# Moving the high half of sixteen weight splits per layer from GpSimd to ScalarE in a two-layer encoder kernel

## The reference

```python
q = (xc @ w_query).reshape(-1, PEER_HEADS, 2, PEER_HALF)
s1, s2 = scores of both halves of q against sub_keys
v1, i1 = lax.top_k(s1, 16); v2, i2 = lax.top_k(s2, 16)
sv, pos = lax.top_k(all 256 sums v1 + v2, 16)
eidx = i1 * 128 + i2 at pos;  gate = softmax(sv)
act = gelu(einsum('thkd,td->thk', u_tab[eidx], xc))
y = einsum('thk,thkd->td', gate * act, v_tab[eidx])
x = layer_norm(ALPHA * x + y)
```

## Time and profile before

| | before |
|---|---|
| median of 3 runs | 3995.9 us (3995.53 to 3997.57) |
| profiled execution, its own time | 3997.35 us |
| its span in the trace | 3995.6 us |
| PE busy | 3807.2 us (95%) |
| DVE busy | 2760.0 us (69%) |
| POOL busy | 2505.9 us (63%) |
| ACT busy | 753.7 us (19%) |
| granted TensorE clock, mean | 0.983 |

### The profile page before, as it was taken

One profiled execution on the slowest core, in us unless ns is written; L12 is line 12 of the kernel. 1 busy time (PEld: TensorE's weight loads), 2 busy tenths in 40 slices (PEclk: granted clock), 3 DMA queues, 4 the chain that ended last, 5 costly groups with the idle time before them and its releaser, 6 DMA issues.

```text
span 3995.6 us, 54149 instructions
## 1 busy us (share of the span) xinstructions
PE 3807.2 (95%) x19024; PEld 3144.7 (79%) x19024; DVE 2760.0 (69%) x3953; ACT 753.7 (19%) x1305; POOL 2505.9 (63%) x1268
## 2 busy tenths in 40 slices
PE   6999996999999999999989999889999999999998
PEld 5778885778878888888877798667788788888886
DVE  7545999996998444444584559999789974444445
ACT  1551112331111111010115401133311110111101
POOL 5435574447777676766654455844577777667674
PEclk9999998999999999999999999999999999999999
DMA  3112234776554333333221123357764543333331
GB/s 143 53 64 93 93 137 140 230 221 235 188 189 158 125 128 116 115 126 120 90 86 64 72 90 111 127 164 220 235 225 178 199 143 121 116 126 126 115 115 74
DMA packets 224634, 546.56 MB, mean 137 GB/s; under 512 B 9728, under 2 KB 141056, under 8 KB 174976
## 3 DMA queue, kind: packets, MB, share of 16 engines
q1 hardware_dynamic: 46656, 335.57, 23.3%
q10 hardware_dynamic: 177856, 209.36, 16.1%
HBM read 442.12 MB, written 102.76 MB: 136 GB/s over the span
## 4 chain that ended last, share of the span: by engine, by line
PE 61%; DVE 30%; issue 6%; DVEq 1%; POOL 1%; ACT 1%; DMA 0%; ACTq 0%; SPq 0%; POOLq 0%
PE bank L1087 19%; PE bank L1089 19%; PE bank L1088 19%; DVE hot L988 3%; DVE Wl L1020 3%; DVE hot2l L993 2%; DVE hot L989 2%; DVE ki L908 2%; DVE Wf L1016 1%; PE bank L1210 1%; DVE pick L951 1%; DVE kv__78 L905 1%; DVE X L1037 1%; DVE pos L908 1%; DVE pick L948 1%
## 5 line engine op out<-in xcount | busy, mean ns | idle before, releaser
L383 POOL TENSOR_TENSOR part_l<-landing,part_h 128x1024 fp32r<-128x1024 f32 x632 | 1705.6, 2699 | 52.8
L380 POOL TENSOR_SCALAR part_h<-landing 128x1024 fp32r<-128x1024 f32 x632 | 810.3, 1282 | 1402.8 <-PE bank L1089 764.1
L1087 PE MATMUL bank<-XTh,part_h 128*128 128x512 f32 (+1 forms) x2688 | 1054.1, 392 | 11.1 <-DVE XTl L711 7.7
L1088 PE MATMUL bank<-XTl,part_h 128*128 128x512 f32 (+1 forms) x2688 | 1038.7, 386 | 0.0
L1089 PE MATMUL bank<-XTh,part_l 128*128 128x512 f32 (+1 forms) x2688 | 1038.4, 386 | 0.0
L1087 PE MATMUL bank<-part_h,Wh 128*128 128x512 f32 x2048 | 800.5, 391 | 9.9 <-DVE X L1037 7.1
L1089 PE MATMUL bank<-part_h,Wl 128*128 128x512 f32 x2048 | 797.3, 389 | 0.0
L1088 PE MATMUL bank<-part_l,Wh 128*128 128x512 f32 x2048 | 797.0, 389 | 0.0
L1087 PEld LDWEIGHTS bank<-XTh,part_h 128*128 128x128 f32 x2688 | 509.6, 190 | 110.0 <-POOL part_l L383 4.4
L1089 PEld LDWEIGHTS bank<-XTh,part_l 128*128 128x128 f32 x2688 | 508.6, 189 | 102.6
L1088 PEld LDWEIGHTS bank<-XTl,part_h 128*128 128x128 f32 x2688 | 509.6, 190 | 97.1 <-issue 0.5
(11 more groups left out here) (165 smaller groups left out, 3542.3 us busy)
## 6 DMA issues: line engine op xcount, KB each, us to landing
landing<-stream SPq DMA_DIRECT2D x316, 1024.0 KB, 4.8
dense_gates<-spill ACTq DMA_DIRECT2D x32, 2048.0 KB, 9.4
gate<-dense_gates ACTq DMA_DIRECT2D x64, 1024.0 KB, 4.8
early_acts<-early ACTq DMA_DIRECT2D x128, 256.0 KB, 2.3
acts_in<-early_acts ACTq DMA_DIRECT2D x32, 1024.0 KB, 7.5
LNP<-ln ACTq DMA_DIRECT2D x5, 1024.0 KB, 4.7
X<-x SPq DMA_DIRECT2D x4, 512.0 KB, 9.7
keyT<-keys ACTq DMA_DIRECT2D x2, 1024.0 KB, 4.8
```

The costliest lines, as they stand in the source:

```text
L380: nc.gpsimd.tensor_scalar(part_h[k][:, w], landing[s][:, w], 1.0, 0.0, ALU.mult, ALU.add).then_inc(high_part, 1)
L383: nc.gpsimd.tensor_tensor(part_l[k][:, w], landing[s][:, w], part_h[k][:, w].bitcast(F32), ALU.subtract).then_inc(split.sem, 1)
L1087: nc.tensor.matmul(dst, sth, mvh, start=first, stop=False)
L1088: nc.tensor.matmul(dst, sth, mvl, start=False, stop=False)
```

## The change

For the sixteen pieces per layer whose splitting falls into the gate stage (pieces P_TAB + 14 to P_TAB + 29 of a layer; P_TAB + 12 is the first used in the stage, and splitting runs two pieces ahead), ACT makes the two high halves and POOL makes only the two low halves. Every piece is still loaded by SP and split in the same two tiles.

```diff
+A_FIRST, A_PIECES = P_TAB + E_BEFORE + 2, E_WITHIN
...
-        high_part = sem("high_part")
+        high_part = tally("high_part", 0, 2 * (NP - A_PIECES))
+        high_within = tally("high_within", 0, 2 * A_PIECES)
...
+            def low_half(s, h):
+                w = slice(h * PIECE // 2, (h + 1) * PIECE // 2)
+                nc.gpsimd.tensor_tensor(part_l[s][:, w], landing[s][:, w], part_h[s][:, w].bitcast(F32),
+                                        ALU.subtract).then_inc(split.sem, 1)
...
+            def low_round(l, r):
+
+                for s in range(LANDINGS):
+                    pool.sem_inc(went_on, 1)
+                    for h in range(2):
+                        pool.wait_ge(high_within.sem, high_within.at(l, r * (2 * LANDINGS) + (2 * s + h + 1 - 2 * A_FIRST)))
+                        low_half(s, h)
+
+            def pieces_of(l):
+                with pool.Fori(1, A_FIRST // LANDINGS) as r:
+                    split_round(l, r, 0)
+                with pool.Fori(A_FIRST // LANDINGS, (A_FIRST + A_PIECES) // LANDINGS) as r:
+                    low_round(l, r)
+                with pool.Fori((A_FIRST + A_PIECES) // LANDINGS, NP // LANDINGS) as r:
+                    split_round(l, r, A_PIECES)
+
+            first_round()
+            pieces_of(0)
+            with pool.Fori(1, DEPTH) as l:
+                split_round(l, 0, 0)
+                pieces_of(l)
...
                             if q % 4 == 3:
                                 early_half(b, 2 * k + q // 4)
+                            if q == 7:
+                                high_ahead(b, 2 * k + 1)
...
+                def high_ahead(b, c):
+
+                    n, s = E_BEFORE + 2 + c // 2, (A_FIRST + c // 2) % SPLITS
+                    act.wait_ge(landed[s], l * (8 * NP) + b * 16 + ((P_TAB + n) // 2 * 16 + 16))
+                    act.wait_ge(used.sem, used.at(l, 2 * b + (P_TAB + n - SPLITS + 1)))
+                    for h in range(2):
+                        w = slice(h * PIECE // 2, (h + 1) * PIECE // 2)
+                        nc.scalar.copy(part_h[s][:, w], landing[s][:, w]).then_inc(high_within.sem, 1)
```

More of the change, by code:

```diff
@@ L45 @@
 E_EXP = 6
+A_FIRST, A_PIECES = P_TAB + E_BEFORE + 2, E_WITHIN
+assert A_FIRST % 2 == 0 and A_PIECES % 2 == 0
 assert E_WITHIN == 2 * (S // 64)
@@ L369, in _, with split_round @@
         def _(pool):
-            def split_round(r, first):
+            def low_half(s, h):
+                w = slice(h * PIECE // 2, (h + 1) * PIECE // 2)
+                nc.gpsimd.tensor_tensor(part_l[s][:, w], landing[s][:, w], part_h[s][:, w].bitcast(F32),
+                                        ALU.subtract).then_inc(split.sem, 1)
+            def split_round(l, r, skipped):
                 for s in range(LANDINGS):
[L372 to L376, removed]
+                    pool.wait_ge(landed[s], l * (8 * NP) + (r * 16 + 16))
+                    pool.wait_ge(used.sem, used.at(l, r * LANDINGS + (s - SPLITS + 1)))
                     pool.sem_inc(went_on, 1)
@@ L379, in split_round @@
                         w = slice(h * PIECE // 2, (h + 1) * PIECE // 2)
[L380 to L384, removed]
@@ L386, in _, with first_round @@
-            split_round(0, True)
-            with pool.Fori(1, DEPTH * NP // LANDINGS) as r:
-                split_round(r, False)
+                        nc.gpsimd.tensor_scalar(part_h[s][:, w], landing[s][:, w], 1.0, 0.0, ALU.mult,
+                                                ALU.add).then_inc(high_part.sem, 1)
+                        pool.wait_ge(high_part.sem, high_part.at(l, r * (2 * LANDINGS) + (2 * (s - skipped) + h + 1)))
+                        low_half(s, h)
+            def first_round():
+                for s in range(LANDINGS):
+                    pool.wait_ge(landed[s], 16)
+                    pool.sem_inc(went_on, 1)
+                    for h in range(2):
+                        w = slice(h * PIECE // 2, (h + 1) * PIECE // 2)
+                        nc.gpsimd.tensor_scalar(part_h[s][:, w], landing[s][:, w], 1.0, 0.0, ALU.mult,
+                                                ALU.add).then_inc(high_part.sem, 1)
+                        pool.wait_ge(high_part.sem, 2 * s + h + 1)
+                        low_half(s, h)
```

## The result

| | before | changed |
|---|---|---|
| median | 3996.74 us (3995.53 to 3998.44, 4 runs) | 3956.85 us (3955.46 to 3957.44, 4 runs) |
| span of the profiled execution | 3995.6 us | 3955.6 us |
| PE busy | 3807.2 us (95%) | 3795.5 us (96%) |
| DVE busy | 2760.0 us (69%) | 2707.6 us (68%) |
| POOL busy | 2505.9 us (63%) | 2421.2 us (61%) |

The changed kernel is faster by 39.9 us; the ratio of the two is 0.990, with a 95% interval of 0.9885 to 0.9916. Forecast were 3962 and a range from 3957 to 3977. The sign and what bounds the stage were forecast rightly; the saving, 33.8 us, was 6 us too small.

The account below looks back on a forecast made before the run. DVE, blocked by POOL, was taken to bound the gate stage, then PE. Stalls lost, 19.5 - 2.6 + 19.4 - 2.5 = 33.8 us, other parts costing nothing, took 3997.35 to 3963.6; as a median 3962, range 3957 to 3977.

Parts of the forecast that it names:

- What bounds the stage: Gate stage before: DVE's one-hot operations set the pace, held up by POOL; 16.34 us per half block against PE's 14.96.
- DVE now: DVE in the gate stage after the change: 14.75 us per half block, 1.59 less than before, 0.21 less than PE needs.
- its idling for the slots: Expected sign in the gate stage: DVE would idle, waiting for PE to use its slots; no size given.
- PE becomes the bound: Gate stage: PE's 3.74 us per step sets the pace, so the gain is PE's stall; 33.8 us saved, chance 0.68.
- The stall that PE loses: PE's waiting in the gate stage before: 19.5 us in the first layer, 19.4 in the second, less 2.6 and 2.5 staying.
- The range: Forecast limits for the whole kernel's median time: 3957 to 3977 us.
- One stall stays: Step 1 of each gate stage: POOL still splits piece P_TAB + 13, costing 2.6 us and 2.5 in the second layer.
- The work added to ACT: Two casts per piece on ACT in the gate stage: 1.06 us each, 2.1 for both, hidden, costing nothing.
- The cover: Gate stage, half block's end: time between ACT's gate copies ending at 5.6 us and PE wanting them at 7.48; 1.9 us.
- Behind the stage: After the gate stage: PE sets the time and passes its gain on; ACT's added 2.1 us lie under a 12.51 us wait.
- the first, DVE the bound in part: Gate stage: low halves wait for whole DVE operations, half block 15.49 us; kernel 3965 to 3984 us, chance 0.19.
- The second, DVE's whole saving: Gate stage: PE could go below 3.74 us per step, 25.4 us saved per layer, kernel 3945 us; chance 0.05.

## Why the prediction was wrong in size and right in kind

- **What bounds the stage**: right. DVE held PE because POOL held DVE; the doubled and the halved high halves moved the stage about as the model of that blocking gives (24.1 and 24.3 us more against some 25; a stage of 250.1 and 249.2 against 249.7).
- **DVE now**: 14.75 us per half block were forecast and 14.82 measured on average (14.67 for the first, 14.9 from step 31 on). The two low halves took 5.74 together for the first piece, and a low half of the stage 2.74 on average, where 2.70 was taken. That step 7 would be ready 1.8 us before PE wants it was right (1.9). DVE's gain on PE per half block, forecast at 0.21, was 0.3 at first, 0.06 at the end and 0.14 on average, and its idling for the slots did not come.
- **PE becomes the bound**: right as a mechanism, every step but step 1 is at 3.74. **The stall that PE loses is the term that was mis-sized.** "First layer: 891.79 + 3.74 - 636.68 = 258.85 us for 64 steps" spans 63 steps. The stall of before was not 19.5 and 19.4 us but 262.6 - 239.4 = 23.2 and 262.5 - 239.4 = 23.1. With them the same sum is 23.2 - 2.6 + 23.1 - 2.5 = 41.2, and the stages gave back 41.2. The median would have been forecast at 3954.7; the three launches of the changed kernel gave 3953.6 to 3956.9. The prediction's own DVE budget could have warned: 16 half blocks of 16.34 us make 261.4, more than the stage it was said to fill.
- **The range**: its lower end, 3957, is what comes out when all 19.5 + 19.4 = 38.9 us of counted stall go, and that sum had the same error in it. It did not count that launches of one kernel differ by some 3 us. With the time 0.15 us outside, this spread alone could have put it on either side of the bound; the 5 us between forecast and time come from the miscount, which is worth 7.4.
- **One stall stays**: right, 6.30 and 6.36 us for step 1, where 6.34 and 6.20 stood before.
- **The work added to ACT**: right. 1.06 was estimated for a cast and 1.05 measured; hidden, as the run without casts shows. The cover was put at 1.9 us and never fell below 3.0: gate copies end at least 3.0 us before PE wants their banks (4.0 before), because the casts fill in part a pause of ACT that was there already (1.58 us idle).
- **Behind the stage**: right. PE passed its gain on. From the second stage's end to the end of the span it is 1116.7 us before and 1116.8 now, and DVE's wait for `Wh` is 12.55 us as before (12.51):

```profile
913.87 4.03 DVE L1066 TENSOR_TENSOR Wl<-Wf,Wh 128x512 fp32r<-128x512 f32 x2 [12.55 <-ACT Wh L667]
```

- **The rivals**: the first, DVE the bound in part, did not come, but its margin was real: one high half left on POOL, or two slots less, bring stalls back. The second, DVE's whole saving, came to 1.52 us per half block on average (16.34 to 14.82), of which PE let 20.6 of 24.3 per layer through. The rule of the Trainium skill named there ("Perfetto Trace Analysis", section "Identifying the Most-Contended Engine") would have left PE headroom at 77% of weight loads. In the run without low halves nothing holds PE back and the loads stand at 49.11 of 60, 82%. So 82% is this stage's ceiling by that measure, and 77% left 6% to gain in those 60 us, not 23. Here the trace does not bear the rule out: the repeated length of a step was the better floor.

## What to carry to other kernels

When an engine that looks idle enough shares time with the engine that sets the pace, look at the length of the latter's operations beside it, not at busy shares: here POOL, busy 44% of the stage, cost DVE 5.86 of every 16.34 us. The gain of such a relief is capped by the next engine's floor, so measure that floor and the stage it fills by counting steps, and check the count against a second budget of the same stretch. An average rate that suffices is not enough where the blocking comes in bursts: the buffers have to hold a burst. And measure a stage from an event that both kernels share: here from DVE's first operation (the same within 0.05 us in three executions), since the first step of PE moved with the clock by up to 1.5 us.

## What the runs showed of the hardware

- A GpSimd operation and a one-hot operation of VectorE with two SBUF inputs go in turn: for every GpSimd operation one of VectorE gets done, 1.53 us beside 1.3 and 2.88 beside 2.7, and 0.68 alone. The Trainium skill, "SBUF — State Buffer", section "Who interferes with whom", names as the cause a read interface shared with GpSimd, through which a VectorE instruction gets its second SBUF input. The rows agree in that both have to wait; the interface itself no row shows.
- ScalarE's casts from the same tile show nothing of it: all 64 took 1.04 to 1.06 us, also beside a low half on POOL and blocked operations on DVE.
- A low half of GpSimd took 2.39 us where DVE had finished, and up to 4.3 beside selections of 2.29 us on 128x2048. In the changed kernel's second launch one that began at 592.12, 1.0 us after a selection, took 4.32, and the selection that began behind it at 594.21 took 4.38: each waited for the one that was there first.
- TensorE's granted clock stood at 0.50 after a wait of 27 us for the routing and rose to 1.00 only while PE worked again: 0.4 us after the first large matmul in one execution, 3.6 us in another. Whether PE's shorter wait in the second (16.8 us) has a part in it is not shown.
